# The four merge-gate jobs of a hybrid decoder layer multiplied by Strassen's scheme, seven half-size products each

## What is computed

```python
def mixer_out(x, gate_ada, f, o_n, o_d, w_up_nsa, w_up_dsa, w_out):
    u_n = (o_n * jax.nn.silu(f['nsa_z'])) @ w_up_nsa
    u_d = (o_d * jax.nn.silu(f['dsa_z'])) @ w_up_dsa
    g_n, g_d = jnp.split(jax.nn.sigmoid(f['merge']), 2, axis=-1)
    return x + gate_ada[:, None, :] * ((g_n * u_n + g_d * u_d) @ w_out)
```

## Time and profile before

| | us |
|---|---|
| median of 3 runs | 620.12 |
| lowest, highest | 618.89, 623.26 |
| profiled execution, its own time | 620.08 |
| its span, first to last instruction | 618.2 |
| mean granted clock of PE in it | 0.986 |

### The profile page before, as it was taken

How to read it: one execution, slowest core, us unless ns; L and a number is a source line. 1 busy time by engine, 2 the same in 40 slices (tenths; PEclk the granted TensorE clock), 3 DMA queues, 4 the chain that set the end, 5 groups by cost and what they waited for, 6 DMA issues and landing times.

```text
span 618.2 us, 12162 instructions
## 1 busy us (share of the span) xinstructions
PE 588.5 (95%) x4630; PEld 483.5 (78%) x4630; DVE 338.3 (55%) x847; ACT 248.0 (40%) x549; POOL 152.0 (25%) x196
## 2 busy tenths in 40 slices
PE   5999999998999999999999999999999999999995
PEld 1587776765776887766775679999999999998784
DVE  1454035968878556878676664433232542227873
ACT  6232255232131345666466554343213232223443
POOL 1126350450350445553554430000000000000130
PEclk9799999999799999999999999999999999999998
DMA  9991731521342264001201306328332242333003
GB/s 321 385 323 31 295 114 39 165 65 56 108 139 83 73 173 139 2 1 50 88 2 49 91 1 169 105 69 268 116 69 70 84 122 69 89 117 137 1 28 118
DMA packets 52426, 68.37 MB, mean 111 GB/s; under 512 B 5089, under 2 KB 34969, under 8 KB 52208
## 3 DMA queue, kind: packets, MB, share of 16 engines
q1 hardware_dynamic: 49744, 56.85, 30.0%
q10 hardware_dynamic: 1808, 6.31, 2.8%
q0 software_dynamic: 816, 4.43, 1.8%
HBM read 62.99 MB, written 6.66 MB: 113 GB/s over the span
## 4 chain that ended last, share of the span: by engine, by line
PE 82%; DVE 9%; SPq 2%; issue 2%; ACT 2%; DMA 2%; POOL 1%; DVEq 0%; ACTq 0%; POOLq 0%
PE psum L1161 30%; PE psum L934 8%; PE psum L936 7%; PE psum L935 7%; PE psum L1423 3%; PE psum L1346 3%; PE psum L1391 3%; PE psum L1261 3%; PE psum L960 2%; PE psum L1068 2%; DVE psum L2079 2%; PE psum L949 1%; DVE score L2003 1%; SPq L714 1%; DVE top L2002 1%
## 5 line engine op out<-in xcount | busy, mean ns | idle before, releaser
L1551 ACT ACTIVATE w_hi<-stage 128x1024 fp32r<-128x1024 f32 (+2 forms) x56 | 56.1, 1002 | 160.5 <-PE psum L1161 93.9
L1893 DVE TENSOR_TENSOR w_lo<-stage,w_hi 128x1024 fp32r<-128x1024 f32 x34 | 41.7, 1225 | 110.5 <-ACT w_hi L1551 107.2
L1161 PE MATMUL psum<-hT_hi,w_hi 128*128 128x272 f32 x368 | 76.4, 289 | 0.0
L1161 PE MATMUL psum<-hT_lo,w_hi 128*128 128x272 f32 x368 | 76.2, 288 | 0.0
L1161 PE MATMUL psum<-hT_hi,w_lo 128*128 128x272 f32 x368 | 75.9, 288 | 0.0
L934 PE MATMUL psum<-w_hi,hT_hi 128*128 128x512 f32 (+3 forms) x192 | 70.3, 366 | 0.7 <-DVE rope_b L1940 0.4
L844 POOL TENSOR_TENSOR w_lo<-stage,w_hi 128x1024 fp32r<-128x1024 f32 (+2 forms) x22 | 44.2, 2011 | 108.6 <-ACT w_hi L1551 108.6
L936 PE MATMUL psum<-w_lo,hT_hi 128*128 128x512 f32 (+3 forms) x192 | 67.4, 351 | 0.0
L935 PE MATMUL psum<-w_hi,hT_lo 128*128 128x512 f32 (+3 forms) x192 | 67.4, 351 | 0.0
L925 POOL TENSOR_TENSOR y<-y,final_g 128x512 f32<-128x512 f32 (+1 forms) x5 | 7.8, 1581 | 217.7 <-ACT merged L1781 217.7
L1161 PEld LDWEIGHTS psum<-hT_hi,w_hi 128*128 128x128 f32 x368 | 57.8, 188 | 0.4 <-DVE w_lo L1893 0.2
(11 more groups left out here) (346 smaller groups left out, 1123.4 us busy)
## 6 DMA issues: line engine op xcount, KB each, us to landing
stage<-in_w_in SPq DMA_DIRECT2D x14, 1024.0 KB, 5.2
stage<-in_w_ada SPq DMA_DIRECT2D x8, 1024.0 KB, 10.3
stage<-in_w_in SPq DMA_DIRECT2D x10, 512.0 KB, 5.2
staging<-in_x_prompt ACTq DMA_DIRECT2D x4, 512.0 KB, 5.4
cached<-in_cache_nsa_kv SPq DMA_DIRECT2D x32, 64.0 KB, 2.2
stage<-in_cache_nsa_kv SPq DMA_DIRECT2D x16, 128.0 KB, 2.1
stage<-in_state_nsa_win_kv SPq DMA_DIRECT2D x2, 1024.0 KB, 6.4
stage<-in_cache_dsa_kv SPq DMA_DIRECT2D x16, 128.0 KB, 2.1
```

The costliest lines, as they stand in the source:

```text
L1161: last = mm(out[:, h, :], left[w][:, k, P * x:P * x + P], halves(mov[m])[:, h, :], start=(k == 0 and w + m == 0), stop=(k == tiles - 1 and ...
L1551: last = A(dst, src, ACT.Copy)
L1893: last = tt(dst, src, hi.bitcast(F32), ALU.subtract)
```

## The change

With weights W and h each cut into 2 x 2 blocks (W: two pairs of output tiles by two halves of the 1024 features; h: two halves of the features by two halves of the tokens), a merge job is a 2 x 2 block product: eight block products before, seven now (Strassen's scheme in Winograd's form). A block product is 2 output tiles x 4 k x 3 terms = 24 matmuls of 272 columns; a job has 168. Consecutive matmuls no longer share weights.

- **Pieces.** A merge job has 7 pieces, one per product (`OPERANDS` gives for each the staged row, the half, and how many weight sums it needs). Four products use sums of weights; DVE makes the four sums in place in the staging slot (`weight_sum`), two of them in the job ahead (`sums_ahead`, z: at its last tile, un and ud: at their third), two in the job.
- **When a slot is free.** Both loads of a merge job are read until late: `pieces_of_load` is 6 for the first and 7 for the second, where it was 2 and 4.
- **Sums of h.** Four, made once: in the z jobs DVE rebuilds four blocks of h from hi and lo (`unsplit`), makes four differences (`sum_whole`), ACT and DVE split them (`high_of_sum`, `low_of_sum`), the last one over a block of `hT` after the last z tile.
- **Products on PE.** `by_seven` runs products 0 to 6 into three pairs of banks u, v, w. Three times ACT copies a pair of banks to memory (`snap`), DVE adds such a copy and a pair of banks (`add`), and ACT takes four sigmoids (`squash`), three from memory.
- **Moved.** The last two merges of the first ud job go into the third merge job (mn, c = 1). The loads of x and `final_g`, and the two spreads of gates, go from the first mn job to the last ud job. `product` gives the un jobs their banks in another order. The memory of the new buffers lies over `silu_z`, `mT` and `y`.

```diff
@@ plan
-PIECES = [2 if k in ("un", "ud") else 4 for k, _ in JOBS]
+BY_SEVEN = [i for i, x in enumerate(JOBS) if x[0] in ("mn", "md")]
+OPERANDS = [(0, 0, 0), (0, 1, 0), (0, 0, 2), (1, 0, 1), (0, 0, 4), (0, 1, 3), (1, 1, 0)]
+
+PIECES = [7 if i in BY_SEVEN else 2 if k in ("un", "ud") else 4 for i, (k, _) in enumerate(JOBS)]
+def pieces_of_load(job, e):
+    return 6 + e if job in BY_SEVEN else 2 * e + 2
@@ SP, wait of a load
-                        sp.wait_ge(lo_made, FIRST[old[1]] + 2 * old[2] + 2)
+                        sp.wait_ge(lo_made, FIRST[old[1]] + pieces_of_load(*old[1:]))
@@ PE
+            def by_seven(job):
...
+                def product(q, out, moving, first, last):
+                    pe.wait_ge(lo_made, n + q + 1)
+                    left = [w_part(x, n + q, 512).rearrange("p (k n) -> p k n", k=4) for x in range(2)]
+                    for tile in range(2):
+                        for k in range(4):
+                            for x, m in ((0, 0), (1, 0), (0, 1)):
+                                done = mm(out[:, tile, :], left[x][:, k, P * tile:P * tile + P], moving[m][:, k, :],
+                                          start=(first and k + x + m == 0), stop=(last and k == 3 and m == 1),
+                                          skip_group_check=True)
+                    done.then_inc(piece_used, 1)
...
+                g_read(pe, g - 1, 0)
+                product(0, u, quarter(0, 0), True, False)
+                g_read(pe, g - 1, 1)
+                product(1, w, quarter(1, 0), True, True)
+                pe.wait_ge(snapped, 3 * at + 1)
+                product(2, u, summed_h(1), False, False)
+                g_read(pe, g - 1, 2)
+                product(3, v, summed_h(0), True, False)
+                pe.wait_ge(snapped, 3 * at + 2)
+                product(4, u, summed_h(2), False, False)
+                pe.wait_ge(snapped, 3 * at + 3)
+                product(5, v, quarter(1, 1), False, True)
+                pe.wait_ge(summed, 3 * at + 2)
+                product(6, u, summed_h(3), False, True)
@@ ACT, by_seven
+                snap(0, partial[:, 0], u)
+                split_hi(n + 2)
+                split_hi(n + 3)
+                snap(2, partial[:, 1], u)
+                split_hi(n + 4)
+                snap(3, partial2[:, :, :], v)
+                if JOBS[job] == ("mn", 1):
+                    merged_high(0, 2)
+                split_hi(n + 5)
+                if JOBS[job] == ("mn", 1):
+                    merged_high(0, 3)
+                squash(0, 0, out_of(job, 0, 0), 1)
+                split_hi(n + 6)
+                split_hi(n + 7)
+                squash(1, 1, out_of(job, 1, 1), 2)
+                split_hi(n + 8)
+                squash(0, 1, out_of(job, 0, 1), 3)
+                act.wait_ge(piece_used, n + 7)
+                squash(1, 0, u, 3)
@@ DVE, job ahead
+            def sums_ahead(job):
+                arrived(dve, ("w", job, 1))
+                weight_sum(job, (1, 0), (1, 0), (1, 1), ALU.add)
+                weight_sum(job, (0, 0), (1, 0), (0, 0), ALU.subtract)
@@ DVE, by_seven
+                weight_sum(job, (0, 1), (0, 1), (0, 0), ALU.subtract)
+                split_lo(n + 2)
+                weight_sum(job, (0, 0), (1, 1), (0, 0), ALU.subtract)
+                split_lo(n + 3)
+                add(1, 0, 0, w, partial[:, 0], 1)
+                split_lo(n + 4)
+                if JOBS[job] == ("mn", 1):
+                    merge(0, 2)
+                split_lo(n + 5)
+                if JOBS[job] == ("mn", 1):
+                    merge(0, 3)
+                add(4, 1, 1, u, partial2[:, :, :], 3)
+                split_lo(n + 6)
+                add(5, 0, 1, v, partial[:, 1], 2)
+                split_lo(n + 7)
+                split_lo(n + 8)
```

More of the change, by code:

```diff
@@ new lines, in by_seven, with add @@
+            def by_seven(job):
+                n, at = FIRST[job], BY_SEVEN.index(job)
+                u, v, w = banks_of(job)
+                def add(q, row, tokens, src, copy, i):
+                    dve.wait_ge(piece_used, n + q + 1)
+                    dve.wait_ge(snapped, 3 * at + i)
+                    own()
+                    tt(out_of(job, row, tokens), src, copy, ALU.add).then_inc(*tell(summed))
+                weight_sum(job, (0, 1), (0, 1), (0, 0), ALU.subtract)
[14 more added lines that the diff above has]
+                split_lo(n + 8)
```

167 lines of the change are left out of this document (140 added, 27 removed).

## The result

The changed kernel takes 652.68 us (median of 4 executions, 649.91 to 654.96), the kernel before 620.55 (4 executions, the three of the table ahead and one more, 618.89 to 623.26). The ratio is 1.051, with a 95% interval of 1.048 to 1.055: 5% slower. The prediction said slower, at 640, with a range up to 652.

A forecast was written before the change was run, and what follows sets the result against it. The prediction took TensorE (PE) to set the pace of the merge and up-projection stage. 620.08 less 12.0 of matmuls, plus 30.9 of stalls with restarts and 1 for sharing of transfers, gave 640 us, range 633 to 652.

The forecast's parts named there:

- What was taken away: Four merge jobs: each does 168 matmuls instead of 192, 12.0 us less PE work.
- New weights at no cost: Weights loaded for every matmul instead of every second: taken as 0, bounded at 0 to 0.003 us per matmul.
- Durations: Instruction times on DVE and ACT from the profile: 1.14 us per 1024-wide DVE operation, 1.21 per 1088-wide sum.
- Step 1: Inside a merge job: snapshots delay high halves, products 2 and 4 late; 0.88 us in each md job, 1.8 in all.
- Step 2: Heads of un and ud jobs: up-projection load issued late because its slot frees late; four stalls, 15.5 us.
- Step 3: Way into the first merge job: DVE's list of work makes products 1, 2 and 4 late; 5.2 us.
- Step 4: Way into the third merge job: DVE's work and two deferred merges delay low halves; 6.2 us together.
- Step 5: z jobs: two sums behind the first tile push a low half back; 0.6 us.
- rival A: The forecast: stalls as worked out, the clock falls once at most; 632 to 647 us, chance 0.56.
- B: Clock falls in several stalls, up to 3.3 us each: two give 646, five 656, six 660; chance 0.32.
- C: Not slower: the up-projection load lands under cover; 623 us, chance 0.05.
- D: The gain arrives: DVE and ACT keep up everywhere; 608 us, chance 0.03.

The follow-up runs named there:

- e9: e5 with the first weight sum of the first merge job back at the fourth z tile; 614.24 us, ratio 0.988.
- e11: Kernel before the change, loop over token halves outermost so that no two matmuls in a row share weights; 622.65 us, ratio 1.002.
- e2: Changed kernel with a third staging slot for the up-projection loads, so they are issued a job ahead; 629.88 us.
- e1: Changed kernel with spare matmuls on old operands while PE waits at the six long stalls; 641.57 us.
- e6: Kernel before the change with each un and ud load issued only when the merge job's last tile begins; 648.49 us.
- e7: e6 with 28 spare matmuls on old operands ahead of the first tile of each un and ud job; 639.47 us.
- e8: e2 with spare matmuls on old operands in the two long stalls it still has; 625.21 us.
- e5: Changed kernel with the slot of e2 and another order of work on ACT and DVE; 616.19 us, ratio 0.990 to 0.995.
- e3: Changed kernel with the 16 weight sums and 8 sums of h on GpSimd instead of DVE; 658.15 us.
- e4: e3 with the slot of e2 and, on ACT, high halves of later pieces ahead of the snapshots; 637.75 us.
- e10: Kernel before the change with late un and ud loads, the four waits filled by 4, 10, 16 and 22 spare matmuls; 645.77 us.

## Why the prediction was right and wrong

**What was taken away** (12.0): right. PE has 96 matmuls fewer, 0.125 apart in a product; e9's stage is shorter by 12.0 less the stalls and gaps counted above. **New weights at no cost**: nearly right, within its bound of 0 to 0.003; e11 has 0.0005 each, 0.3 us for the 672 matmuls that are concerned.

**Durations.** A little low. The forecast needs the time from start to start. A low half gives 1.14 as taken, but the instruction behind a weight sum starts 1.25 to 1.26 later, not 1.14, and behind a 1088-wide one 1.32 to 1.39 later, not 1.21 and just over the bound of 1.3. Their recorded lengths are 1.22 and 1.29.

**Step 1**: the mechanism right, the size a little low, 1.16 instead of 0.88 for each job.

**Step 2**: right in every part: the issue 2.90 us after product 4 began (2.98), 8.09 to ACT's start (7.95), four stalls of 15.8 in all (15.5), and e2 takes them away with the slot and nothing else.

**Step 3**: the place right, 6.1 for 5.2. Product 1's term was half its size (0.6 for 1.19); 0.2 of that is the two weight sums ahead of its low half, at 1.25 each.

**Step 4**: 6.0 for 6.2, though product 2 had no stall of its own; it is hidden behind product 1's, which was 0.4 longer.

**Step 5**: 1.1 for 0.6. The forecast push is the 0.64 at the first z job's last tile. The 0.42 at the tile before it was not forecast: ACT began that tile's high half 3.94 us into the stage, where the kernel before has 3.61; e1 and e2, with the same order there, have 3.75 and 3.67 and no such stall.

**The sum of the stalls**, 30.9, was measured at 32.2, or 33.8 with the small gaps. The 1 us for sharing was not seen apart.

**The clock** is the step that failed: the choice of rival A ("the clock falls once at most", 0.56) over B (0.32). All six stalls of 2.9 us and more brought a fall, and e1 gives 11.1 of the 12.7 us between 640 and 652.7 to them. My argument against B was that a stall of 4 us is hardly longer than the 3.5 us between PE's last work and the fall at 615, so some may pass. That read the row wrongly: it shows one delay from the end of work to a fall and says nothing on how much shorter it can be. e6 to e7 show the same without the change. The Trainium skill (TensorE: Matmul & The Clock Gate, Why this matters for your kernels) advises against idle gaps of PE between bursts of matmuls, because its clock goes back to half. The trace agrees: the clock fell at all six stalls, of which the shortest had 2.89 us. B deserved more than half of the chances.

B's term was mis-sized too. I took up to 3.3 us for each fall, about half of 6.8 us, the only slow stretch with PE at work that the earlier trace rows show; at six falls that gives 660. Four of the six stretches lasted only 3.4 us, and what is lost is somewhat less than half of the part in which PE works: 1.4 us of the stretch of 3.4 shown above, 2.5 of that of 6.8, whose first 1.4 us lie in the stall. The runs give 1.85 (e1), 2.35 (e8 to e2) and 2.25 (e7 to e6) for each. Six at 1.85 on top of the forecast are 651, between the fastest and slowest measured execution.

**The rivals.** C, a load that lands under cover, was put at 623 for the stalls that stay without step 2. e8 is that case without falls: 625.2, step 2 gone by another slot. Alone it is no gain; D's 608 needs the order too, and e9 comes to 614.2.

**The signs named ahead**: PE's gaps of 4 us at the up-projection jobs, the issue 3 us after product 4, the waits of 4 and 3 us for DVE and the distance of 0.125 came as named. Of the clock it was said that it would be 1.00 but after such gaps; inside the gate stage that is what happened, after each of them.

## What to carry to other kernels

A change that saves matmuls is paid for at the heads of jobs: ask for every staging slot who its last reader is now, and for every engine what stands ahead of the operand that TensorE wants next; here a slot of its own and another order turned 5% slower into 1% faster with the same work. Count a stall of TensorE as long as those here (2.9 us and more) at its length plus some 2 us of clock, and before moving sums to GpSimd, look whether VectorE reads two operands from SBUF beside it. When work is moved forward, check that its data has landed by then (e5 lost 3 us to a sum that waited for a load).

## What the runs showed of the hardware

- **Stalls and the clock.** In the gate stages of all runs, 24 stalls of PE had 2.89 to 5.28 us, and behind or in each of the 24 the granted clock went to 0.50 (1.2 GHz), for 3.4 or 6.8 us. Of four stalls of 2.0 to 2.53 us one (2.00, in e3) had a fall and three (2.00 in e4, 2.52 in e3, 2.53 in e10) had none; of nine of 1.4 to 1.85 none. Between 2.53 and 2.89 nothing was tried. In a slow stretch matmuls of 272 columns begin 0.227 us apart instead of 0.125.
- **Falls without a long stall.** Ahead of the gate stage the clock fell near 155 us in 10 of the 13 profiled executions and near 220 in 8, in variants of both kernels. No pause of PE there is above 1.23 us, and in the 7.2 us before the fall at 223.2 of the changed kernel PE is busy throughout (7.20 of 7.20). What brings these is not shown; they come and go between executions.
- **GpSimd and VectorE.** A sum of 128 x 1024 on POOL took 2.55 us on average beside a working DVE, and DVE's subtractions of the same size went from 1.225 to 1.56 on average, 2.35 for those that ran beside a sum; ACT's copies stayed at 1.06.
- **An up-projection load** of two transfers took 7.8 to 8.6 us from its issue until ACT started (four loads each in the changed kernel, e6 and e7; eleven of the twelve at most 8.2), in the kernel before (made late) as in the changed one, where 1 MB of `w_in` in one transfer has a median of 5.5 to its landing.
